# Stick-breaking attention: both heads of a key block in one slot of the program, instead of one head after the other

## The reference

```python
z = jnp.einsum('bhqd,bhkd->bhqk', q[:, :, qs:ke], k[:, :, :ke]).astype(jnp.float32) * scale
mask = s_pos < t_pos
log_keep = jnp.where(mask, -jax.nn.softplus(z), 0.0)
suffix = lax.cumsum(log_keep, axis=3, reverse=True) - log_keep
attn = jnp.where(mask, jnp.exp(jax.nn.log_sigmoid(z) + suffix), 0.0)
outs.append(jnp.einsum('bhqk,bhkd->bhqd', attn.astype(v.dtype), v[:, :, :ke]))
```

## Time and profile before

| | us |
|---|---|
| median of three runs | 3397.34 |
| the profiled execution | 3399.04 |
| its span, first to last instruction | 3397.2 |
| group 0's mixer alone, up to the first gather | 381 |
| of it stick(0), from its first to its last product | about 59 to 132 |
| stick(1) beside the ring, from its q projection on | about 488 to 740 |
| stick(2) beside the ring | about 1350 to 1783 |

### The profile page before, as it was taken

How to read it: one execution, slowest core, us unless ns; L and a number is a source line. 1 busy time by engine, 2 the same in 40 slices (tenths; PEclk the granted TensorE clock), 3 DMA queues, 4 the chain that set the end, 5 groups by cost and what they waited for, 6 DMA issues and landing times.

```text
span 3397.2 us, 40650 instructions
## 1 busy us (share of the span) xinstructions
PE 2260.1 (67%) x13656; PEld 1211.1 (36%) x13656; DVE 2178.7 (64%) x4954; ACT 1229.7 (36%) x3176; POOL 1189.1 (35%) x1065
## 2 busy tenths in 40 slices
PE   7888758996996674888877798575653333333333
PEld 4665634453553442343434354242321111111111
DVE  3511666657555788766786765578886666666654
ACT  2210136545431234665872453222421232132211
POOL 1100123333332333443444433334444444444443
PEclk8978879997998897998888799887775665656565
DMA  8623769898999998999999999999999999999997
GB/s 325 207 80 114 266 275 372 354 367 319 360 400 378 412 372 335 417 410 402 388 417 395 420 418 418 421 419 407 414 398 421 421 421 421 421 420 419 421 418 303
DMA packets 202469, 1254.18 MB, mean 369 GB/s; under 512 B 23098, under 2 KB 29274, under 8 KB 71187
## 3 DMA queue, kind: packets, MB, share of 16 engines
q0 software_dynamic: 152224, 1090.81, 78.6%
q1 hardware_dynamic: 50036, 160.77, 12.5%
HBM read 1236.27 MB, written 15.22 MB: 368 GB/s over the span
## 4 chain that ended last, share of the span: by engine, by line
DMA 28%; PE 22%; DVE 18%; issue 5%; ACT 5%; POOL 0%; DVEq 0%; POOLq 0%; SPq 0%; ACTq 0%
DMA ring<-in_uv,idx 27%; PE pb L934 8%; DVE ring L1589 8%; PE pb L860 4%; PE pb L867 2%; PE pb L787 2%; PE pb L757 1%; ACT L974 1%; ACT wts L1191 1%; DVE kidx L1500 1%; DMA wst<-in_w_all 1%; PE pb L880 1%; DVE zone L1502 1%; DVE kidx L1506 1%; DVE vals L1504 1%
## 5 line engine op out<-in xcount | busy, mean ns | idle before, releaser
L643 POOL DMA_INDIRECT ring<-in_uv,idx x1024 | 1169.0, 1142 | 2061.5 <-PE pb L934 1614.9
L1589 DVE CUSTOM_DVE_ANT_0 ring<-h2r,ring 128x1024 f32<-128x1024 f32 x1024 | 1232.2, 1223 | 551.2 <-DMA ring<-in_uv,idx 546.1
L934 PE MATMUL pb<-ring,wts 128*32 128x256 f32 x8192 | 746.2, 527 | 886.1 <-ACT wts L1191 886.1
L934 PEld LDWEIGHTS pb<-ring,wts 128*32 128x32 f32 x8192 | 308.8, 144 | 1295.6 <-ACT wts L1191 1032.0
L1188 ACT ACTIVATE gl<-dots 128x4 f32<-128x4 f32 x256 | 52.5, 205 | 1203.8 <-DVE dots L1589 1202.9
L974 ACT ACT_TABLE_LOAD x226 | 290.0, 1283 | 4.8 <-PEq L1741 0.7
L914 PE MATMUL pb<-zone,wst 128*128 128x384 f32 (+1 forms) x768 | 248.9, 481 | 0.8 <-issue 0.8
L1191 ACT ACTIVATE wts<-gm,gl 128x32 f32<-128x32 f32 x1024 | 245.1, 310 | 8.5
L914 PEld LDWEIGHTS pb<-zone,wst 128*128 128x128 f32 x768 | 153.6, 206 | 91.3 <-issue 27.1
L860 PE MATMUL pb<-hT,wst 128*128 128x384 f32 x512 | 170.8, 490 | 0.7 <-ACT ys L1105 0.7
L1340 DVE SCALAR_TENSOR_TENSOR zone<-pb,zone 128x384 f32<-128x384 f32 (+2 forms) x120 | 57.0, 476 | 148.7 <-ACT zone L1028 145.9
(11 more groups left out here) (179 smaller groups left out, 2745.7 us busy)
## 6 DMA issues: line engine op xcount, KB each, us to landing
wst<-in_w_all SPq DMA_DIRECT2D x148, 512.0 KB, 8.1
ring<-in_w_all SPq DMA_DIRECT2D x50, 512.0 KB, 4.5
wst<-in_w_ada POOLq DMA_DIRECT2D x32, 512.0 KB, 5.8
ring<-in_uv,idx POOLq DMA_INDIRECT x1024, 14.6
ring<-in_w_ada SPq DMA_DIRECT2D x16, 512.0 KB, 11.7
ys<-mod_scratch SPq DMA_DIRECT2D x9, 512.0 KB
zone<-in_x SPq DMA_DIRECT2D x8, 512.0 KB, 4.3
hT<-in_x SPq DMA_DIRECT2D x8, 512.0 KB, 11.8
```

What stands on the lines that cost most here:

```text
L643: pool.indirect_dma_start(ring[:, n % RING, :], None, uv, bass.IndirectOffsetOnAxis(ap=idx4[:, piece % 2, col:col + 1], axis=0)).then_inc( ...
L934: m = pe.matmul(pb[32 * f:32 * f + 32, 6 + q // 2, (q % 2) * 256:(q % 2 + 1) * 256], wts[:, n % WBUFS, :], ring[:, n % RING, D + 256 * f:D ...
L1589: dve.tensor_tensor_reduce(u, h2r[:, q, :], u, 1.0, 0.0, ALU.mult, ALU.add, dots[:, n % 16:n % 16 + 1]).then_inc(dots_done, 1)
```

## The change

`chunks_of` lists the two heads of a key block one behind the other, and every step takes both in one slot: a slot with an even number (within a pair of heads) has `scores` and `values` of two chunks each, one with an odd number `logarithm`, `suffix` and `attention` of two; `softplus` and `running` stand in even slots. The number of slots stays. In `scores` the two products stand one behind the other (head 0 on the array's rows 0 to 63, head 1 on rows 64 to 127), and then the two masks. `values` has the two heads one behind the other too, on columns 0 to 63 and 64 to 127. ACT takes `logarithm` ahead of `attention` in a slot. The running sums get a fourth buffer and `att` a fourth, since two heads are under way. The weights of `plan` for a chunk fall from 1.1, 2.0 and 1.0 to 0.8, 2.0 and 0.6.

```diff
-ZBANKS, DEEP, ATTS = 4, 4, 3
+ZBANKS, DEEP, ATTS, LATER = 4, 4, 4, 4
...
-    return [(e, s, (max(s, a) - a) * P, (b - a) * P) for e in range(2) for s in reversed(range(b))]
+    return [(e, s, (max(s, a) - a) * P, (b - a) * P) for s in reversed(range(b)) for e in range(2)]
...
-def chunk_at(g, s):
+def chunks_at(g, s):
 
     t, i = divmod(s, 2 * GROUPS[g][1] + 2)
-    return (t, i) if 0 <= t < SB_PAIRS and i < 2 * GROUPS[g][1] else None
+    return [(t, i), (t, i + 1)] if 0 <= t < SB_PAIRS and i < 2 * GROUPS[g][1] and i % 2 == 0 else []
...
-        for delay, cost in ((0, 1.1), (3, 2.0), (4, 1.0)):
-            c = chunk_at(g, s - delay)
-            if c:
-                w += cost * (0.2 + 0.8 * (chunks[c[1]][3] - chunks[c[1]][2]) / 384.0)
+        for delay, cost in ((0, 0.8), (3, 2.0), (4, 0.6)):
+            for t, i in chunks_at(g, s - delay):
+                w += cost * (0.2 + 0.8 * (chunks[i][3] - chunks[i][2]) / 384.0)
...
-                        need(pe, att_done, c - ZBANKS + 1)
-                        m = pe.matmul(pb[:, c % ZBANKS, 0:hi - lo], kT[64 * e:64 * e + 64, s * P:(s + 1) * P],
-                                      qT[64 * e:64 * e + 64, lo:hi], start=True, stop=True)
+                        need(pe, att_done, c + 1 - ZBANKS + 1)
+                        for e in range(2):
+                            m = pe.matmul(pb[:, (c + e) % ZBANKS, 0:hi - lo], kT[64 * e:64 * e + 64, s * P:(s + 1) * P],
+                                          qT[64 * e:64 * e + 64, lo:hi], start=True, stop=True)
+                            if s < a:
+                                m.then_inc(z_done, 1)
                         if s >= a:
-                            m = pe.matmul(pb[:, c % ZBANKS, 0:P], ident_b[:], unseen_b[:], start=False, stop=True, skip_group_check=True)
-                        m.then_inc(z_done, 1)
+                            for e in range(2):
+                                pe.matmul(pb[:, (c + e) % ZBANKS, 0:P], ident_b[:], unseen_b[:], start=False, stop=True, skip_group_check=True).then_inc(z_done, 1)
...
-                        if chunk_at(g, s - 3):
-                            suffix(*chunk_at(g, s - 3))
-                        if chunk_at(g, s - 4):
-                            values(*chunk_at(g, s - 4))
+                        for c in chunks_at(g, s - 3):
+                            suffix(*c)
+                        for c in chunks_at(g, s - 4):
+                            values(*c)
...
-                        if chunk_at(g, s - 3):
-                            attention(*chunk_at(g, s - 3))
-                        if chunk_at(g, s - 1):
-                            logarithm(*chunk_at(g, s - 1))
+                        for c in chunks_at(g, s - 1):
+                            logarithm(*c)
+                        for c in chunks_at(g, s - 3):
+                            attention(*c)
...
-                            need(dve, later_done, l)
-                            op = dve.tensor_tensor(later[l % 3][:, first:hi], later[(l - 1) % 3][:, first:hi], spl[c % DEEP][:, first - lo:hi - lo], ALU.add)
+                            need(dve, later_done, l - 1)
+                            op = dve.tensor_tensor(later[l % LATER][:, first:hi], later[(l - 2) % LATER][:, first:hi], spl[c % DEEP][:, first - lo:hi - lo], ALU.add)
```

More of the change, by code:

```diff
@@ L386, in build @@
         qT = z(2 * S, TMAX)
-        later = [z(2432 + i * TMAX, TMAX) for i in range(3)]
-        spl = [z(3584 + i * TMAX, TMAX) for i in range(DEEP)]
-        att = [z(3584 + (DEEP + i) * TMAX, TMAX) for i in range(ATTS)]
+        later = [z(2432 + i * TMAX, TMAX) for i in range(LATER)]
+        spl = [z(2432 + (LATER + i) * TMAX, TMAX) for i in range(DEEP)]
+        att = [z(2432 + (LATER + DEEP + i) * TMAX, TMAX) for i in range(ATTS)]
         qb = z(0, 4, TMAX)
@@ L711, in scores @@
                     def scores(t, i):
-                        e, s, lo, hi = chunks[i]
+                        s, lo, hi = chunks[i][1:]
                         c, pair = CHUNK_BASE[g, t] + i, SB_PAIRS * g + t
@@ L731, in suffix @@
                         if first < hi:
-                            l = LATER_BASE[g, t] + later_index(g, i - 1)
+                            l = LATER_BASE[g, t] + i - 2
                             pe.wait_ge(later_done, l + 1)
-                            m = pe.matmul(pb[:, c % ZBANKS, first - lo:hi - lo], negones[:], later[l % 3][:, first:hi], start=False, stop=True, skip_group_check=True)
+                            m = pe.matmul(pb[:, c % ZBANKS, first - lo:hi - lo], negones[:], later[l % LATER][:, first:hi], start=False, stop=True, skip_group_check=True)
                         m.then_inc(sums_done, 1)
@@ L773, in stick @@
                                 project(pair_at(g, s + 2 - i), i)
-                        if chunk_at(g, s):
-                            scores(*chunk_at(g, s))
+                        if chunks_at(g, s):
+                            scores(*chunks_at(g, s)[0])
                         yield
@@ L1352, in running @@
                         if first < hi:
-                            need(dve, later_done, l)
-                            op = dve.tensor_tensor(later[l % 3][:, first:hi], later[(l - 1) % 3][:, first:hi], spl[c % DEEP][:, first - lo:hi - lo], ALU.add)
+                            need(dve, later_done, l - 1)
+                            op = dve.tensor_tensor(later[l % LATER][:, first:hi], later[(l - 2) % LATER][:, first:hi], spl[c % DEEP][:, first - lo:hi - lo], ALU.add)
                         if s >= a:
-                            op = dve.tensor_copy(later[l % 3][:, lo:lo + P], spl[c % DEEP][:, 0:P])
+                            op = dve.tensor_copy(later[l % LATER][:, lo:lo + P], spl[c % DEEP][:, 0:P])
                         op.then_inc(later_done, 1)
                     for s in stick_slots(g):
-                        if chunk_at(g, s - 2):
-                            softplus(*chunk_at(g, s - 2))
-                            running(*chunk_at(g, s - 2))
+                        for c in chunks_at(g, s - 2):
+                            softplus(*c)
+                            running(*c)
                         t = pair_at(g, s - 2)
@@ L1660, in _ @@
                     final(NB - 1, k)
-def later_index(g, c):
-    b = GROUPS[g][1]
-    e, i = c // b, c % b
-    return e * (b - 1) + i
 def later_made(g, c):
-    b = GROUPS[g][1]
-    return sum(i % b < b - 1 for i in range(c + 1))
+    return max(0, min(c + 1, 2 * (GROUPS[g][1] - 1)))
 def last_tile(piece):
```

4 lines of the change are left out of this document (2 added, 2 removed).

## The result

The changed kernel took 3416.18 us (median of 5 runs, 3414.11 to 3422.39); the kernel before, on the same chip in the same rounds, took 3397.34 (5 runs, 3391.38 to 3399.76). The ratio is 1.0065 [1.0053, 1.0077]: slower, by 18.8 us between the medians, where 20 us faster was forecast, and outside the range of 3352 to 3401. The profiled execution took 3416.18 with a span of 3414.4.

A forecast was written before the change was run, and what follows sets the result against it. PE was taken to bound stick(0) and nearly stick(1), the ring's DMA transfers stick(2). Savings of 14 us in stick(1), 4 in stick(2) and 2 in stick(0), together 20, gave 3377 us; range 3352 to 3401.

The forecast's parts named there:

- Halves side by side: PE's scores and values: second head free on the array's other half, saving 8, 27 and 47 us in groups 0, 1, 2.
- my price for a gap: PE standing between suffix and values for ACT: 1.2 us per wide key block, about 2.5 for 128 and 256 columns.
- The added wait: PE's values wait for ACT's attention behind six logarithm activations: 15 us in stick(1), bounds 0 to 30; 44 in stick(2).
- Waits that go: Stick(1), PE: half the old waits, suffix for softplus 11.8 and values for attention 3.8, vanish, 8 us.
- The rest: Fewer table loads, softplus, transfers and tiles moved behind the sticks, 2.64 us each: nothing, with 5 us to either side.
- My own second step: Priced PE's added waits for ACT at fixed places in the sticks: 15 us in stick(1), 44 in stick(2).
- my third: Table of steps: four and twelve tiles move behind the sticks at 2.64 us each, saving as much as they cost.
- The sum: Savings, waits and DMA's free share together: 14 us in stick(1), 4 in stick(2), 2 in stick(0), 20 in all.
- a flat 418 to 421: GB/s from about 2000 us on, read as all that the DMA engines give, so nothing to save there.
- The fourth: Rival: array halves run one after the other, nothing is saved and gaps stay: 3409 us, chance 0.06.
- The third: Rival: the block of ACT work delays `weigh` and starves the ring in stick(2): 3422 us, chance 0.08.
- The second: Rival: ACT eats the gain, no gap is covered, stick(1) saves 5 us, the others 0: 3392 us, chance 0.22.

The follow-up runs named there:

- e1: The changed kernel with `values` of a key block one slot later, behind the next key block's suffix: 3388.9 us, ratio to before 0.9983.
- e4: The changed kernel with the old weights 1.1, 2.0 and 1.0 in `plan`: 3382.8 us, ratio to before 0.9963.
- e3: The kernel before with only the new weights 0.8, 2.0 and 0.6 in `plan`: 3395.0 us, ratio to before 0.9995.
- e10: The kernel before with only larger weights, 1.3, 2.6 and 1.3, in `plan`: 3381.6 us, ratio to before 0.9963.
- e9: The changed kernel with only larger weights, 1.3, 2.6 and 1.3, in `plan`: 3368.0 us, ratio to before 0.9920.
- e5: As e4, but PE alternates values and scores of the two heads, so no halves run side by side: 3408.7 us, ratio to before 1.0044.
- e12: The changed kernel with weights 1.3, 2.6 and 1.3 in group 1 (stick(1)) only: 3392.6 us, ratio to before 0.9987.

## Why the prediction was wrong, step by step

**Halves side by side: right.** "For scores (row halves) ... I take 0.84" for both heads: the trace has 0.92 to the end of two where one took 0.91. Scores and values of stick(1) were to fall from 64 to 37 to 40 us; they fell to 42.3. Where values have not to wait for two attentions one after the other, as in e1, they are halved to the microsecond: 92.8 us busy before, over the whole program, and here

```profile
L749 PE MATMUL pb<-zone 128*64 128x384 f32 (+2 forms) x240 | 46.5, 461 | 1.5 <-ACT zone L1038 1.5
```

In the changed kernel the second head's `values` still waits for its own attention: the two take 1.15 us at a granted clock of 1.00 (the row of 1416.95 above), where one alone took 0.86. That is one part of the excess. PE's clock is another; how much each makes in all was not added up. In the timeline above, directly behind the wait of 7.53 us, the same two groups of products take 1.92 and 1.65 us instead of 1.15 and 0.92. The granted clock before, in and behind that wait:

```profile
1395.00:1400.00 5.00, 5.00 (x45) 2.69 (x44) 4.82 (x11) 1.37 (x6) 2.36 (x2) 0.99 1.01 415
1400.00:1407.00 7.00, 0.14 (x1) 0.00 (x0) 6.79 (x13) 5.16 (x9) 3.94 (x3) 0.88 1.02 424
1407.00:1411.00 4.00, 3.33 (x8) 1.08 (x8) 3.82 (x7) 3.92 (x10) 0.00 (x0) 0.50 1.02 424
```

PE had stood from 1400.1 to 1407.7. The products that follow pay for the wait once more, here with 1.92 + 1.65 - 1.15 - 0.92 = 1.5 us, which my price for a gap left out.

**The added wait: the mechanism right, the size twice too small in stick(1).** Forecast 15 us in stick(1) and 44 in stick(2); measured 33.0 and, from 1350 to 1800, 55.8. The step priced a slot as if ACT had only the logarithm ahead of attention. The timeline of ACT in these waits shows what else it did: in stick(1) about 14 of the 33.0 us are the ring's `weigh`, its table loads and ACT's own wait for the dot products, nearly all in the three longest waits; in stick(2) about 11 of the 55.8, table loads above all. Without these about 19 and 44 us are left. In e4, whose wait in stick(1) is the same 32.9 us, the ring's share is only some 6, so there the assumption that failed is that the ring's products cover half of the gaps. The bound I gave, 30, was passed a little.

**Waits that go: right in kind.** Suffix for softplus was 11.8 us in stick(1) and is 2.0, so 9.8 us went, where 8 were forecast for it and values' 3.8 together; the latter did not go but is part of the 33.0.

**"The rest", the table of steps: this is the step that failed.** It says "as much is saved before as is paid after: nothing, with 5 us to either side." Measured on the changed order it is 33 us (e4 to changed). It would have been right for the order before, where e3 is no different from before, though not for more tiles: e10 gains 13 us there. The step took the time of a stage to be that of its tiles, 2.64 us each, from a stretch where DMA is the bound, and applied it to both sides. Inside the changed stick a tile costs far less: from the changed kernel to e9, 38 more tiles made the two sticks 37.9 us longer, 1.0 each, all of it in stick(2), and none in stick(1), which takes 218 to 221 us beside 64, 69 or 76 tiles; from e3 to e10, in the old order, 39 made them 66.2 longer, 1.7 each. Outside the sticks a tile is worth 2.0 to 2.3 us on average in both: (48.2 + 37.9) / 38 and (13.3 + 66.2) / 39. The old order gains little from a tile more or less, since price inside and outside are near each other; the new order has PE's long waits, in which the ring's work is free in stick(1), and loses about a us and a quarter for each tile taken out. My own second step, which put fixed waits into the stage, contradicts my third, which let the stage shrink with its tiles; I did not hold them against each other.

**The sum.** With the old table, the only one for which the sum can be read by itself, the order alone gives 13 us where 20 were forecast. Stick(1) is 5.0 us shorter (forecast 14) and stick(2) 4.8 (4). The gathers begin 5.7 us earlier (2), but stick(0) itself is only 0.7 us shorter, and 3.1 of the 5.7 lie ahead of its first product, where the kernels do not differ: that part is luck, not the change's. Stick(1) is off because its wait was forecast too small. With the new table the same order makes stick(1) 11 us longer than e3's, so beside that table the sum fails in the stage that it rests on most.

One reading of the rows was too smooth, without consequence for the sum: from about 2000 us on they are not "a flat 418 to 421", but hold 407, 414 and 398 in slices 28 to 30 and 303 in the last.

**The rivals.** The fourth (halves one after the other) is refuted by 0.92 and by e5, though its 3409 is only 7 us from the measured time. The third put slower at 3422, nearest of all with 6 us, by starving the ring in stick(2); with the same order e4 and e9 feed it at 409 and 415 GB/s, so the order alone does not do that, and half of the loss against e9 lies in stick(1)'s table (e12). The second, ACT eating the gain, is in part true for stick(1), and gives 3392; with the table's 33 us on top the time would be 3425. The rival that was missing is a stage too short in tiles for its own fixed length.

**What is open.** Later values gain 27 us at 36 and 73 half quads, 6 at 42 and 85 (3368.0 to 3362.5, on different chips and not clear of noise), and nothing at 38 and 79; the three sticks, stick(0) included, are 19, 11 and 9 us shorter, so their lengths do not explain these times. The table shifts every meeting of ring and stick, and no run separates that from the plain count of tiles. Nor was it tried what more than four banks would give, and no run tells why 8 tiles more behind stick(2) cost 27 us.

## What to carry to other kernels

When work that was bound by an engine becomes bound by waits for other engines, the share of other work laid beside it has to be measured again. Here it had to go up: a cheaper step was no reason to give its stage fewer tiles, since stick(1) did not get shorter by what it no longer carried. Split such a change into its order and its weights, and measure each alone. A wait removed in front of one instruction is a gain only if the stage, from its first to its last product, gets shorter.

## What the runs showed of the hardware

Two float32 products of 384 columns on row halves of the array end 0.92 us after the first begins, where one alone takes 0.91; of 256 and 128 columns on two halves, 0.70 and 0.49 us in stick(0), like one alone:

```profile
56.87 0.49 PE L720 MATMUL pb<-zone 64*128 64x128 f32 x4
...
57.51 0.70 PE L720 MATMUL pb<-zone 64*128 64x256 f32 x4
```

The second half of the rows is free at each of these three widths. The column halves of `values` are too: 46.5 us for 92.8, as shown above for e1. The Trainium skill (TensorE: Matmul & The Clock Gate, "Measured speedup vs the span model") has 2.38 times for three column parts, 0.79 of the ideal; two parts here reach the ideal of two.

The change between kinds of product costs about a tenth of a us, as the prediction estimated and left out. A suffix product of 384 columns, on the whole array, is followed after 0.65 us by another on the whole array, here from 1414.19 to 1414.84:

```profile
1414.19 0.81 PE L737 MATMUL pb<-zone,negones 128*128 128x384 f32 x2
1414.84 0.81 PE L732 MATMUL pb<-zone,tri 128*128 128x384 f32 x2
```

Where `values`, on 64 columns of the array, comes next it is 0.74, from 1396.70 to 1397.44; where another kind stood ahead, 0.75 (1395.95 to 1396.70).

The granted clock was 0.99 before the wait of 7.53 us in stick(2), and 0.50, 1.2 instead of 2.4 GHz, over the products behind it (the rows are above). It came back while PE worked on, and the wait of 0.66 us that followed did not lower it:

```profile
1411.00:1413.00 2.00, 2.00 (x30) 1.04 (x32) 1.05 (x3) 1.97 (x3) 0.00 (x0) 0.72 0.60 242
1413.00:1419.00 6.00, 5.29 (x28) 2.15 (x20) 5.68 (x13) 5.80 (x13) 5.00 (x4) 1.00 0.75 250
```

In e5 products of 384 columns took 1.65 us at such a place and 0.91 elsewhere, so its 26 us need not be the price of the halves alone.
